# A fused two-block transformer on one core: the sparse attention's chain placed between its projection chunks, with convolution and weight splitting in one block ahead of the attention units

## Chip, cores and metric

The kernel runs on one core of a Trainium2 chip as a single launch. The metric is the device time of one execution in microseconds. Every number of a trace below is from one profiled execution; TensorE, VectorE, ScalarE and GpSimd are its compute engines, SP issues the weight loads.

## What is computed

The reference runs twelve stages on 256 tokens of width 1024: neighbourhood attention, dilated attention, a recurrent mixer with retention, two cross-attentions to a memory, a sparse attention with a short convolution, and six gated feed-forward layers, each between RMS norms. The change lies in the sparse attention stage. Cut to what matters:

```python
p = rms_norm(x) @ w_in      # 256 c_q | 128 c_kv | 64 k_idx | 8 w_idx | 3 x 512 h, gate_b, gate_c
c_q, c_kv = rms_norm_2(c_q, gq), rms_norm_2(c_kv, gkv)
q = einsum('btr,rhd->bthd', c_q, w_uq)
q_lat = einsum('bthd,hdc->bthc', q, w_uk)
q_idx = einsum('btr,rhd->bthd', c_q, w_qi)
score = einsum('bth,bths->bts', w_idx * 512 ** -0.5, relu(einsum('bthd,bsd->bths', q_idx, k_idx)))
# keep the 64 causal keys of highest score, softmax over them, values are c_kv
o = einsum('bthc,hcd->bthd', attend(q_lat, c_kv, top64(score)), w_uv)
u = gate_c * h                                   # short convolution, 3 taps over time
y = gate_b * (w0 * u[t-2] + w1 * u[t-1] + w2 * u[t] + b)
out = concat([o, y]) @ w_out
```

## The kernel before

**Weights.** All weight matrices lie in one stream of chunks of 128 x 2048 floats (1 MB). SP loads chunk after chunk into three slots of `raw`. ScalarE rounds a chunk to `whi` (`act_hi`, line 299; the "high part"), VectorE computes `wlo = raw - whi` (`dve_lo`, line 306; the "low part"; `half_lo`, line 312, does half of one). A product of full precision is then three matmuls: high x high, high weight x low input, low weight x high input (`mm3`, lines 230 to 232, and `mm3t`, lines 236 to 238, with the operands swapped). The slots are reused in a ring: ScalarE may write the high part of chunk c + 3 when TensorE has finished chunk c (`w_used`), VectorE then writes its low part and signals `w_lo`, for which TensorE waits before that chunk, and for which SP waits before it loads chunk c + 6 into `raw`.

**A stage.** Each stage has a projection (the chunks' products go to three banks `pj` in turn, VectorE evacuates a bank, scales it by the norm `rP` and frees it with `pj_free`), its own middle, and an output product `out_pe` over chunks with all four `acc` banks, followed by the post norm (`post_dve`) and the next stage's pre norm. `slices_pe` computes the first two chunks of a projection while the pre norm is still being made.

**The order of work** is written out by hand: each engine has a function that issues its instructions one after another (`pe_f`, `dve_f`, `act_f` of `dsa`), and counters of semaphores tie them together.

**The sparse attention stage** (`dsa`, lines 1223 to 1475). A projection chunk holds two tiles of 128 output columns, `tile_fm` for each half. Its nine chunks are: 0 and 1 (the three tiles of `c_q` and `c_kv` in `CQ`, and the index key written twice as `CK`), 2 (a tile with only eight columns, the index weights `WI`, by `few_tm`, and the first tile of `h`), 3 to 7 and the first half of 8 (the rest of `HB`: `h`, `gate_b`, `gate_c`). Behind the last of them comes a chain:

- ScalarE's squares `C2` (line 1430) are summed over partitions by TensorE with a column of ones (lines 1279, 1282); VectorE makes the variances (1357, 1358), GpSimd the roots (2300), TensorE spreads them (1287), VectorE normalises `CQ` (1374).
- TensorE makes index queries (1295) and the transposed keys (1301); ScalarE copies them out (1432); eight times TensorE makes two heads' index products (1311), ScalarE the ReLU (1445), VectorE the weighted sum into `SC` (1389, 1391).
- TensorE makes head queries (1295) and latent queries (1319), ScalarE copies them (1432, 1452).
- VectorE adds the causal mask (1397), takes the top 8 and replaces them eight times (1401, 1403) for two tiles of queries, and writes the mask `MBs` (1404, 1405).
- Between these, VectorE computes the short convolution: `gate_c * h` (1370), and for each of four tiles four operations (`conv`, 1363 to 1366); ScalarE makes the high parts of the result for the output product (1460).

Then `attn_pe`, `attn_dve` and `attn_act` run eight attention units (two heads and 128 queries each): scores, softmax, transposes of the weights, values. Their first scores wait for the mask. VectorE's `for k in range(8)` behind them (line 1412) makes the low parts of the output operand, four from the convolution and four from the attention's output (1332), which TensorE computes behind the first output chunk. The output product starts with the convolution's tiles. ScalarE issues the loads of the memory for the next stage (`mem_load`) ahead of the units.

## Time and profile before

| what | value |
|---|---|
| median of 3 runs | 2087.94 us |
| lowest, highest | 2085.4, 2097.81 us |
| the profiled execution's own time | 2086.02 us |
| its span, first to last instruction | 2084.2 us |
| mean granted TensorE clock | 0.983 |
| TensorE busy | 2003.8 us, 96% |
| VectorE busy | 1387.5 us, 67% |
| ScalarE busy | 944.2 us, 45% |
| chain that ended last | TensorE 86%, VectorE 9%, ScalarE 2% |

The page of a profile gives busy times by engine, a row of 40 equal slices of the span for each engine, and the chain of work that ended last. The granted clock is the share of TensorE's full speed. A timeline lists instructions in order of time; the idle time before one and what ended it stand in brackets. A table of stretches gives each engine's busy time between two moments. Matmuls overlap, so an instruction's length (0.28 us for a 256-column one) is longer than the distance to the next (0.11 us).

### The profile page before, as it was taken

The numbers are of one execution on the slowest core, as the hardware profiler recorded it, in microseconds if no ns is written. First come the engines' busy times: TensorE is split into PE (matmuls) and PEld (weight loads), VectorE is DVE, ScalarE is ACT, GpSimd is POOL, SyncE is SP. The second block draws the span as 40 slices with busy tenths as digits, with TensorE's granted clock in tenths as the row PEclk, the third lists the DMA queues.
The fourth block names the chain that finished last, engine by engine and source line by source line (L and its number), as shares of the span: only waits on it lengthen the run. The fifth ranks groups of instructions, "written<-read, shape, count | busy, mean of one in ns | idle before, by whom it ended". The sixth has DMA issues, their size and how long they took to land.

```text
span 2084.2 us, 37138 instructions
## 1 busy us (share of the span) xinstructions
PE 2003.8 (96%) x15066; PEld 1860.1 (89%) x15066; DVE 1387.5 (67%) x1853; ACT 944.2 (45%) x1258; POOL 33.2 (2%) x48
## 2 busy tenths in 40 slices
PE   7999999999999999999997999999999996999998
PEld 7879988999979988998997888998899895898997
DVE  6867756666767756775677575776577457666774
ACT  4554444443554444444344354444444443644442
POOL 0000000000000000000000010000000000000000
PEclk9999999999999999999999889999999998999999
DMA  7434564444415464555530223456455643143553
GB/s 299 153 115 182 198 214 173 179 162 152 153 72 202 182 225 151 200 183 211 205 131 16 87 93 131 171 192 215 159 193 190 219 177 134 52 162 112 189 201 124
DMA packets 49788, 341.46 MB, mean 164 GB/s; under 512 B 5776, under 2 KB 6544, under 8 KB 9616
## 3 DMA queue, kind: packets, MB, share of 16 engines
q1 hardware_dynamic: 45216, 321.21, 42.8%
q10 hardware_dynamic: 4464, 18.68, 2.4%
q8 instruction: 84, 1.38, 0.3%
q14 instruction: 24, 0.20, 0.0%
HBM read 338.82 MB, written 1.05 MB: 163 GB/s over the span
## 4 chain that ended last, share of the span: by engine, by line
PE 86%; DVE 9%; ACT 2%; issue 1%; POOL 0%; DMA 0%; DVEq 0%; SPq 0%; POOLq 0%; ACTq 0%
PE pj L230 15%; PE pj L232 15%; PE pj L231 15%; PE acc L236 7%; PE acc L238 7%; PE acc L237 7%; PE pj L236 2%; PE pj L238 2%; PE pj L237 2%; PE pj L571 2%; DVE wlo L306 2%; PE pj L577 1%; PE acc L638 1%; PE acc L651 1%; PE mb L662 1%
## 5 line engine op out<-in xcount | busy, mean ns | idle before, releaser
L306 DVE TENSOR_TENSOR wlo<-raw,whi 128x2048 fp32r<-128x2048 f32 x285 | 652.3, 2291 | 279.2 <-ACT whi L299 278.2
L230 PE MATMUL pj<-xh,whi 128*128 128x256 f32 x2704 | 753.3, 279 | 14.0 <-DVE wlo L316 12.8
L299 ACT ACTIVATE whi<-raw 128x2048 fp32r<-128x2048 f32 x299 | 569.6, 1911 | 399.1 <-PE acc L238 177.9
L231 PE MATMUL pj<-xl,whi 128*128 128x256 f32 x2704 | 749.5, 277 | 0.0
L232 PE MATMUL pj<-xh,wlo 128*128 128x256 f32 x2704 | 749.3, 277 | 0.0
L230 PEld LDWEIGHTS pj<-xh,whi 128*128 128x128 f32 x2704 | 510.1, 189 | 18.9 <-issue 15.5
L231 PEld LDWEIGHTS pj<-xl,whi 128*128 128x128 f32 x2704 | 509.8, 189 | 0.1
L232 PEld LDWEIGHTS pj<-xh,wlo 128*128 128x128 f32 x2704 | 509.7, 188 | 0.0
L236 PE MATMUL acc<-whi,AR 128*128 128x512 f32 x656 | 256.9, 392 | 2.4 <-DVE AR L777 2.3
L237 PE MATMUL acc<-whi,AR 128*128 128x512 f32 x656 | 255.8, 390 | 0.0
L238 PE MATMUL acc<-wlo,AR 128*128 128x512 f32 x656 | 255.7, 390 | 0.0
L832 ACT ACTIVATE AR<-F 128x256 f32 (+1 forms) x132 | 55.2, 418 | 374.4 <-DVE F L813 374.4
L236 PEld LDWEIGHTS acc<-whi,AR 128*128 128x128 f32 x656 | 123.6, 188 | 28.7 <-DVE AR L777 2.8
L238 PEld LDWEIGHTS acc<-wlo,AR 128*128 128x128 f32 x656 | 123.4, 188 | 25.9
L237 PEld LDWEIGHTS acc<-whi,AR 128*128 128x128 f32 x656 | 123.5, 188 | 25.1
L816 DVE TENSOR_TENSOR AR<-F,AR 128x256 f32 (+1 forms) x132 | 56.1, 425 | 100.8 <-ACT AR L832 100.8
L805 DVE TENSOR_TENSOR F<-pj,rP 128x512 f32<-128x512 f32 x132 | 90.4, 685 | 0.7
L236 PE MATMUL pj<-whi,xh 128*128 128x256 f32 (+1 forms) x304 | 85.8, 282 | 0.1
L238 PE MATMUL pj<-wlo,xh 128*128 128x256 f32 (+1 forms) x304 | 84.9, 279 | 0.0
L237 PE MATMUL pj<-whi,xl 128*128 128x256 f32 (+1 forms) x304 | 84.9, 279 | 0.0
L571 PE MATMUL pj<-xh,whi 128*128 128x256 f32 x320 | 82.4, 292 | 0.0
L571 PE MATMUL pj<-xh,wlo 128*128 128x256 f32 x320 | 78.1, 278 | 0.0
(358 smaller groups left out, 2355.3 us busy)
## 6 DMA issues: line engine op xcount, KB each, us to landing
raw<-in_wstream SPq DMA_DIRECT2D x302, 1024.0 KB, 4.8
F<-in_gains ACTq DMA_DIRECT2D x12, 512.0 KB, 4.3
F<-in_rpb ACTq DMA_DIRECT2D x3, 1024.0 KB, 4.8
XM<-in_memtok ACTq DMA_DIRECT2D x2, 1024.0 KB, 4.8
XM<-in_memin ACTq DMA_DIRECT2D x2, 1024.0 KB, 6.9
F<-in_small ACTq DMA_DIRECT2D x1, 1536.0 KB, 10.4
F<-in_xin SPq DMA_DIRECT2D x2, 512.0 KB, 6.1
xt<-in_xtok SPq DMA_DIRECT2D x1, 1024.0 KB, 12.0
```

Source lines behind the costliest of these rows:

```text
L230: nc.tensor.matmul(o, wh, k_hi, start=first, stop=False, skip_group_check=True)
L231: nc.tensor.matmul(o, wh, k_lo, start=False, stop=False, skip_group_check=True)
L232: return nc.tensor.matmul(o, wl, k_hi, start=False, stop=last, skip_group_check=True)
L236: nc.tensor.matmul(o, k_hi, wh, start=first, stop=False, skip_group_check=True)
L237: nc.tensor.matmul(o, k_lo, wh, start=False, stop=False, skip_group_check=True)
L238: return nc.tensor.matmul(o, k_hi, wl, start=False, stop=last, skip_group_check=True)
L299: nc.scalar.activation(whi[:, gs, :], raw[:, gs, :], ACT.Copy).then_inc(w_hi, 1)
L306: nc.vector.tensor_tensor(wlo[:, gs, :], raw[:, gs, :], whi[:, gs, :].bitcast(F32), ALU.subtract).then_inc(w_lo, 1)
L571: nc.tensor.matmul(o, a[:, (w.g + c) % 3, wk], xh[:, k, :], start=k == 0 and half == 0 and i == 0, stop=False, skip_group_check=True)
L805: nc.vector.tensor_tensor(GU.rearrange("p (a t) -> p a t", a=2), pj[ps][:, :].rearrange("p (a t) -> p a t", a=2), rP[:, None, :].to_broadc ...
L816: nc.vector.tensor_tensor(AR[:, bass.ds(c + FT, 1), :] if not isinstance(c, int) else AR[:, c + FT, :], M, (AR[:, bass.ds(c, 1), :] if not ...
L832: nc.scalar.activation(AR[:, bass.ds(c, 1), :] if not isinstance(c, int) else AR[:, c, :], M, ACT.Copy).then_inc(sg(tag, "hi2"), 1)
```

## The change

The projection has eight chunks. The index key (64 columns) and the index weights (8 columns) share one tile, `CR`, which is evacuated like the others; four small matmuls with slices of the identity take the key (once for each half of the partitions) and the weights out of it. `few_tm` is gone, and so is the ninth chunk, of which only a half was used.

The chain is issued by `behind(c, half)` between the halves of chunks 2 to 7: sums and extraction behind the first half of chunk 2, roots behind the first half of chunk 3, index queries behind chunk 3, two of the eight index products behind each half of chunks 4 and 5, head queries behind chunk 6, latent queries behind chunk 7. VectorE's and ScalarE's sequences are written out to match: evacuations (`evac`), low parts (`low`, for the chunk three ahead), scores, and the evacuations of chunks 6 and 7 behind the third and sixth top-8 round. The index products use the `acc` banks.

Between the mask and the softmax of the attention units, VectorE runs one block: the gate product, the four convolutions (their first operation is now ScalarE's, an Identity with scale and bias), the low parts of the first two output chunks in halves, and three low parts of the output operand. The low part of the third output chunk and the fourth of the operand follow the units.

```diff
-    return {"na": 12, "ffn": FT, "dil": 36, "rwrt": 15, "xa": 6, "dsa": 9}[kind]
+    return {"na": 12, "ffn": FT, "dil": 36, "rwrt": 15, "xa": 6, "dsa": 8}[kind]
...
-            dst_tiles = [CQ[:, 0], CQ[:, 1], CQ[:, 2], CK, None] + [HB[:, i] for i in range(12)] + [None]
+            dst_tiles = [CQ[:, 0], CQ[:, 1], CQ[:, 2], CR] + [HB[:, i] for i in range(12)]
...
+                def sums():
+                    pe.wait_ge(S("sq"), 3)
...
+                    for rows in (slice(0, 64), slice(64, 128)):
+                        nc.tensor.matmul(acc[1][rows, T:2 * T], ident[:, 0:64], CR, start=True, stop=True)
+                    for t in range(2):
+                        last = nc.tensor.matmul(acc[1][:, 8 * t:8 * t + 8], CR[:, t * P:(t + 1) * P], ident[:, 64:72],
+                                                start=True, stop=True)
+                    last.then_inc(S("st"), 1)
...
+                def behind(c, half):
+                    if (c, half) == (2, 0):
+                        sums()
+                    elif (c, half) == (3, 0):
+                        roots()
+                    elif (c, half) == (3, 1):
+                        index_queries()
+                    elif c in (4, 5):
+                        v_ = 4 * (c - 4) + 2 * half
+                        logits(v_)
+                        logits(v_ + 1)
+                    elif (c, half) == (6, 1):
+                        head_queries()
+                    elif (c, half) == (7, 1):
+                        latent()
+
+                slices_pe(pe, w)
+                for c in range(2, 8):
+                    pe.wait_ge(w_lo, w.g + 1)
+                    pe.wait_ge(pj_free, w.p + 1)
+                    for half in range(2):
+                        last = tile_fm(pj[w.p % 3], half, w.g % 3)
+                        if half:
+                            last.then_inc(w_used, 1)
+                        behind(c, half)
+                    w.g += 1
+                    w.p += 1
...
+                def evac(c):
                     dve.wait_ge(w_used, w.g + 1)
...
+                def low(c):
+                    dve_lo(dve, g0 + c, (g0 + c) % 3)
+
+                def low_half(c, part):
+                    if part == 0:
+                        dve.wait_ge(w_hi, g0 + c + 4)
+                        half_lo(dve, (g0 + c) % 3, 0)
+                    else:
+                        half_lo(dve, (g0 + c) % 3, 1).then_inc(w_lo, 1)
...
+                def conv(k):
+                    y = hb[:, k, :]
+                    dve.wait_ge(S("qlc"), 5 + k)
+                    link(dve, nc.vector.scalar_tensor_tensor(y, U[:, k, 1:T + 1], v("cw1", k), y, ALU.mult, ALU.add))
+                    link(dve, nc.vector.scalar_tensor_tensor(y, U[:, k, 2:T + 2], v("cw2", k), y, ALU.mult, ALU.add))
+                    nc.vector.tensor_tensor(y, y, bb[:, k, :], ALU.mult).then_inc(S("cv"), 1)
...
+                evac(0)
+                evac(1)
+                low(0)
+                dve.wait_ge(S("st"), 1)
+                link(dve, nc.vector.tensor_scalar(nt[:, 0:2], mb[:, 508:510], 1.0 / 256, EPS, ALU.mult, ALU.add))
+                nc.vector.tensor_scalar(nt[:, 2:4], mb[:, 510:512], 1.0 / 128, EPS, ALU.mult, ALU.add)\
+                    .then_inc(S("mv"), 1)
+                low(1)
+                evac(2)
+                low(2)
+                dve.wait_ge(S("bc"), 1)
...
+                dve.wait_ge(S("cn"), 3)
+                evac(3)
+                low(3)
+                nc.vector.memset(SC[:, 0, P:T], 0.0)
+                nc.vector.memset(U[:, :, 0:2], 0.0)
+                dve.wait_ge(S("qc"), 1)
+                score(0)
+                score(1)
+                evac(4)
+                score(2)
+                score(3)
+                low(4)
+                score(4)
+                score(5)
+                evac(5)
+                score(6)
+                score(7)
...
+                    if n in (2, 5):
+                        evac(6 if n == 2 else 7)
...
+                dve.wait_ge(pj_free, 3 + w.p)
+                nc.vector.tensor_tensor(U[:, :, 2:T + 2], cb_, hb, ALU.mult).then_inc(S("mask"), 1)
+                dve.wait_ge(S("mask"), 2)
+
+                def beside_units(i):
+                    if i < 4:
+                        conv(i)
+                    else:
+                        low_half(5 + (i - 4) // 2, i % 2)
+                        if i > 4:
+                            out_low(i - 5)
+
+                for i in range(8):
+                    beside_units(i)
+                attn_dve(dve, tag, units, 0, lambda grp: None)
+                out_low(3)
+                low(7)
+                for k in range(4, 8):
+                    out_low(k)
...
+                high = lambda: act_phase(act, w, 1, is_proj=True)
+                p0 = w.p
+                high()
+                high()
+                act.wait_ge(pj_free, 3 + p0 + 2)
+                for k in range(3):
+                    nc.scalar.activation(C2[:, k, :], CQ[:, k, :], ACT.Square).then_inc(S("sq"), 1)
+                act.wait_ge(S("st"), 2)
+                nc.scalar.activation(CK, acc[1][:, T:2 * T], ACT.Copy)
+                nc.scalar.activation(WI.rearrange("p a t -> p (a t)"), acc[1][:, 0:16], ACT.Copy, scale=512 ** -0.5)\
+                    .then_inc(S("qc"), 1)
+                high()
+                high()
+                act.wait_ge(S("q"), 1)
...
+                for v_ in range(4):
+                    relu(v_)
+                high()
+                for v_ in range(4, 8):
+                    relu(v_)
+                high()
+                high()
                 act.wait_ge(S("q"), 3)
                 copy_q(QT[:, 0:2], acc[1])
                 copy_q(QT[:, 2:4], acc[2])
+                high()
...
+                def beside_units(i):
+                    if i >= 4:
+                        k = i - 4
+                        act.wait_ge(S("cv"), k + 1)
+                        nc.scalar.activation(AR[:, 4 + k, :], hb[:, k, :], ACT.Copy).then_inc(S("oh"), 1)
+
+                mem_load(act, nmt)
+                act.wait_ge(S("mask"), 2)
                 for k in range(4):
-                    nc.scalar.activation(AR[:, 4 + k, :], hb[:, k, :], ACT.Copy).then_inc(S("oh"), 1)
-                mem_load(act, nmt)
+                    nc.scalar.activation(hb[:, k, :], U[:, k, 0:T], ACT.Identity, scale=v("cw0", k), bias=v("cb", k))\
+                        .then_inc(S("qlc"), 1)
+                for i in range(8):
+                    beside_units(i)
...
-    return ([fm_tile(W, 0), fm_tile(W, P), fm_tile(W, 2 * P), fm_tile(np.concatenate([kidx, kidx], axis=1), 0),
-             fm_tile(pad(W[:, 448:456]), 0)] + [fm_tile(W, 456 + i * P) for i in range(12)]
-            + [np.zeros((P, D), np.float32)])
-
+    return ([fm_tile(W, 0), fm_tile(W, P), fm_tile(W, 2 * P),
+             fm_tile(pad(np.concatenate([kidx, W[:, 448:456]], axis=1)), 0)] + [fm_tile(W, 456 + i * P) for i in range(12)])
```

On TensorE, before, the chain's first matmuls stand behind the last half chunk of the projection (`mb`, `acc`: accumulator banks; `cst`: constants; `F_51`: the stage's working memory; `nt`: the small tile of the variances and roots):

```order
L230 MATMUL pj<-xh,whi 128x256
L231 MATMUL pj<-xl,whi 128x256
L232 MATMUL pj<-xh,wlo 128x256
L1279 MATMUL mb<-cst,F_51 128x1 x4
L1282 MATMUL mb<-cst,F_51 128x1 x2
L1287 MATMUL acc<-cst,nt 128x128 x4
L1295 MATMUL acc<-F_51 128x256 x4
L1295 MATMUL pj<-F_51 128x256 x4
L1301 MATMUL mb<-cst,F_51 128x128 x2
L1311 MATMUL pj<-F_51 128x128 x3
```

In the change, the sums stand behind the first half of chunk 2, with the new extraction (lines 1276, 1278), and the next half chunk follows:

```order
L230 MATMUL pj<-xh,whi 128x256
L231 MATMUL pj<-xl,whi 128x256
L232 MATMUL pj<-xh,wlo 128x256
L1269 MATMUL mb<-cst,F_51 128x1 x4
L1272 MATMUL mb<-cst,F_51 128x1 x2
L1276 MATMUL acc<-F_51,cst 64x256 x2
L1278 MATMUL acc<-cst,F_51 128x8 x2
L230 MATMUL pj<-xh,whi 128x256
L231 MATMUL pj<-xl,whi 128x256
L232 MATMUL pj<-xh,wlo 128x256
```

What moved: the sums went from behind 12 half tiles to behind the first of them; the roots (line 1287, now 1285) come two half chunks later instead of next.

On VectorE, before, from the last low part of the projection to the normalised queries:

```order
L306 TENSOR_TENSOR wlo<-raw,whi 128x2048
L1357 TENSOR_SCALAR nt<-mb 128x2
L1358 TENSOR_SCALAR nt<-mb 128x2
L1368 MEMSET F_51 128x128
L1369 MEMSET F_51 128x4x2
L1370 TENSOR_TENSOR F_51<-F_51 128x4x256
L1363 TENSOR_SCALAR F_51<-F_51,vecs 128x256
L1364 SCALAR_TENSOR_TENSOR F_51<-F_51,vecs 128x256
L1365 SCALAR_TENSOR_TENSOR F_51<-F_51,vecs 128x256
L1366 TENSOR_TENSOR F_51<-F_51 128x256
L1374 SCALAR_TENSOR_TENSOR F_51<-F_51,vecs,acc 128x256 x3
```

In the change, from the first evacuation behind the pre norm to the clearing of `SC` and `U` (line 1372 is the evacuation, 297 the low part, 1421 and 1422 the variances, 1429 the normalised queries):

```order
L1372 TENSOR_TENSOR F_51<-pj,rP 128x256 x4
L297 TENSOR_TENSOR wlo<-raw,whi 128x2048
L1421 TENSOR_SCALAR nt<-mb 128x2
L1422 TENSOR_SCALAR nt<-mb 128x2
L297 TENSOR_TENSOR wlo<-raw,whi 128x2048
L1372 TENSOR_TENSOR F_51<-pj,rP 128x256 x2
L297 TENSOR_TENSOR wlo<-raw,whi 128x2048
L1429 SCALAR_TENSOR_TENSOR F_51<-F_51,vecs,acc 128x256 x3
L1372 TENSOR_TENSOR F_51<-pj,rP 128x256 x2
L297 TENSOR_TENSOR wlo<-raw,whi 128x2048
L1435 MEMSET F_51 128x128
L1436 MEMSET F_51 128x4x2
```

What moved: variances and normalisation now stand between evacuations and low parts; the convolution has left this place.

On VectorE, before, the mask's last two operations (1404, 1405) and the first units' softmax (1255 scales and masks the scores, 692 takes the row maxima):

```order
L1404 TENSOR_SCALAR F_51<-F_51 128x512
L1405 SCALAR_TENSOR_TENSOR F_51<-F_51 128x512
L1255 SCALAR_TENSOR_TENSOR Sb<-acc,F_51 128x256 x2
L692 TENSOR_REDUCE sm<-Sb 128x2
L1255 SCALAR_TENSOR_TENSOR Sb<-pj,F_51 128x256 x2
L692 TENSOR_REDUCE sm<-Sb 128x2
```

In the change, the end of the block ahead of the units: the last convolution (1406 to 1408), the half low parts (303) with those of the output operand (1414), and then the softmax (1247, 683):

```order
L1406 SCALAR_TENSOR_TENSOR F_51<-F_51,vecs 128x256
L1407 SCALAR_TENSOR_TENSOR F_51<-F_51,vecs 128x256
L1408 TENSOR_TENSOR F_51<-F_51 128x256
L303 TENSOR_TENSOR wlo<-raw,whi 128x2x512 x2
L1414 TENSOR_TENSOR AR<-F_51,AR 128x256
L303 TENSOR_TENSOR wlo<-raw,whi 128x2x512
L1414 TENSOR_TENSOR AR<-F_51,AR 128x256
L303 TENSOR_TENSOR wlo<-raw,whi 128x2x512
L1414 TENSOR_TENSOR AR<-F_51,AR 128x256
L1247 SCALAR_TENSOR_TENSOR Sb<-acc,F_51 128x256 x2
L683 TENSOR_REDUCE sm<-Sb 128x2
```

What moved: convolution, gate product, four half low parts and three of the operand's low parts stand between the mask and the first softmax.

## Rows read from the trace of the kernel before

**Rows 1.** Page: granted clock in 40 slices; one DMA issue.

```profile
PEclk9999999999999999999999889999999998999999
...
F<-in_small ACTq DMA_DIRECT2D x1, 1536.0 KB, 10.4
```

**Rows 2.** Stretches of the attention stage; first row names the columns.

```profile
core 0: us, PE busy (x) PEld busy (x) DVE busy (x) ACT busy (x) POOL busy (x), PEclk, DMA share, GB/s
1688.30:1701.70 13.40, 13.34 (x75) 13.26 (x75) 6.34 (x8) 4.19 (x6) 0.00 (x0) 0.62 0.72 277
1701.70:1731.40 29.70, 29.70 (x264) 29.70 (x263) 16.47 (x19) 11.53 (x6) 0.00 (x0) 1.00 0.46 170
1731.40:1741.80 10.40, 3.53 (x23) 3.15 (x21) 9.01 (x16) 1.91 (x1) 2.08 (x1) 0.67 0.59 225
1741.80:1761.60 19.80, 16.56 (x82) 12.07 (x82) 16.46 (x45) 6.76 (x21) 0.00 (x0) 0.92 0.00 0
1761.60:1772.00 10.40, 0.01 (x1) 0.00 (x0) 9.51 (x35) 3.28 (x8) 0.00 (x0) 0.69 0.51 202
1772.00:1796.80 24.80, 24.45 (x148) 21.34 (x149) 18.28 (x52) 15.08 (x43) 0.00 (x0) 0.92 0.00 1
```

**Rows 3.** TensorE timeline: start, length, engine, line, tiles, count [idle before <-releaser].

```profile
1732.22 0.58 PE L1282 MATMUL mb<-cst,F 128*128 128x1 f32 x4
...
1738.33 2.08 PE L1287 MATMUL acc<-cst,nt 128*128 128x128 f32 x8 [5.52 <-POOL nt L2300]
...
1752.35 1.25 PE L1311 MATMUL pj<-F 64*128 64x256 f32 x5 [0.29 <-ACT F L1445]
...
1753.75 3.72 PE L1295 MATMUL acc<-F 128*128 128x256 f32 x16
...
1758.65 2.96 PE L1319 MATMUL acc<-F 64*128 64x256 f32 x16 [1.18 <-ACT F L1432]
...
1772.05 2.05 PE L638 MATMUL acc<-F 128*128 128x256 f32 x4 [10.44 <-DVE F L1405]
...
1796.81 0.47 PE L236 MATMUL acc<-whi,AR 128*128 128x512 f32 x1
```

**Rows 4.** VectorE timeline, chain and mask.

```profile
1736.18 1.21 DVE L1370 TENSOR_TENSOR F<-F 128x1024 f32<-128x1024 f32 x1
...
1741.74 0.41 DVE L1363 TENSOR_SCALAR F<-F,vecs 128x256 f32<-128x256 f32 x1
...
1743.57 0.41 DVE L1363 TENSOR_SCALAR F<-F,vecs 128x256 f32<-128x256 f32 x1
...
1749.32 0.29 DVE L1389 TENSOR_SCALAR F<-F 128x128 f32<-128x128 f32 x1 [2.02 <-ACT F L1445]
...
1756.43 0.69 DVE L1397 TENSOR_TENSOR F<-F 128x512 f32<-128x512 f32 x1
...
1770.76 0.43 DVE L1404 TENSOR_SCALAR F<-F 128x512 f32<-128x512 f32 x1
...
1774.21 0.76 DVE L1255 SCALAR_TENSOR_TENSOR Sb<-acc,F 128x256 f32<-128x256 f32 x2 [2.31 <-PE acc L638]
```

**Rows 5.** VectorE timeline, behind the projection chunks.

```profile
1707.13 0.76 DVE L1351 TENSOR_TENSOR F<-pj,rP 128x256 f32<-128x256 f32 x2 [1.19 <-PE pj L232]
...
1709.09 2.29 DVE L306 TENSOR_TENSOR wlo<-raw,whi 128x2048 fp32r<-128x2048 f32 x1 [1.20 <-ACT whi L299]
...
1712.58 0.75 DVE L1351 TENSOR_TENSOR F<-pj,rP 128x256 f32<-128x256 f32 x2 [1.19 <-PE pj L232]
```

**Rows 6.** ScalarE timeline.

```profile
1687.75 3.71 ACT L299 ACTIVATE whi<-raw 128x2048 fp32r<-128x2048 f32 x2 [5.13 <-PE pj L577]
...
1692.68 1.03 ACT L1430 ACTIVATE F<-F 128x256 f32<-128x256 f32 x3 [1.23 <-DVE F L1351]
...
1763.58 1.35 ACT L1460 ACTIVATE AR<-F 128x256 fp32r<-128x256 f32 x4
```

More of the change, by code:

```diff
@@ L1227, in dsa @@
             C2 = take(3, T)
+            CR = take(T)
             CK = take(T)
@@ L1339, in dve_f @@
             def dve_f(dve, w):
-                for c in range(9):
+                g0 = w.g
+                def evac(c):
                     dve.wait_ge(w_used, w.g + 1)
@@ L1383, in dve_f, with score @@
+                def score(v_):
                     t, a = divmod(v_, 4)
```

169 lines of the change are left out of this document (59 added, 110 removed).

## The prediction, made before the changed kernel had run

> **What bounds the kernel now.** I read the page first, for where TensorE is short of work; then the table of stretches around the sparse attention stage; then the timelines of TensorE, VectorE and ScalarE there. All times below are microseconds of the profiled run's own clock.
>
> The page's row of granted clock [rows 1] stands at nine tenths or more except in three slices. The last of them holds the sparse attention stage. The stretches [rows 2] show it: after two projection chunks, the third takes 13.4 (1688.3 to 1701.7) at a granted clock of 0.62; the next 29.7 are dense at full clock; then come 10.4 with TensorE busy 3.5, 19.8 with 16.6 of small matmuls, 10.4 with nothing at all, and 24.8 of attention units. The last weight matmul of the projection ends at 1731.4 and the first one of the output product starts at 1796.8 [rows 3], so the chain and the units take 65.4.
>
> What ends last in that stretch alternates. TensorE waits 5.52 for GpSimd's roots and later 10.44 for the mask [rows 3]. The mask is VectorE's: eight rounds of top-8 and replace run from 1757.1 (behind the causal addition) to 1770.76, 13.6 or 1.70 a round, and another 1.3 passes until TensorE restarts at 1772.05 [rows 3, 4]. The softmax of unit 0 starts at 1774.21 [rows 4], and 22.6 later the output product starts.
>
> **Part by part: the projection.** A chunk takes 5.44 at full clock: evacuations behind consecutive chunks start at 1707.13 and 1712.58 [rows 5]; half a chunk is 2.72. Before, chunk 2 held the narrow product (48 matmuls of 8 columns) and a full half, and took 13.4; five chunks followed and a last half (2.7), together 43.1. Now six full chunks follow chunk 1: 6 x 5.44 = 32.6. That is 10.5 less weight work, of which the half clock made about half. The price is that the chain's matmuls now stand between the halves, so I walk TensorE from 1688.4.
>
> First half of chunk 2 to 1691.1. Then TensorE waits for the three squares: ScalarE's two conversions start at 1687.75 and take 3.71, and the squares 1.03 [rows 6], so to 1692.5. A stall of 1.4 that was not there. The sums of squares took 1.4 (1731.4 to 1732.8) [rows 3]. New: two 64-row matmuls of 256 columns and two of 8 columns that take the index key and weights out of one tile. The trace has no such pair; sixteen passes of a plain 256-column product take 3.72, 0.46 a matmul [rows 3], so 0.9 and 0.1 for the narrow ones is my upper end, and half of that the lower one if the two row halves overlap. I take 1.0.
>
> Then the rest, each from its row: the roots' spreading took 2.08 at half clock [rows 2, 3], 1.0 at full; the index queries 3.7 and two transposes 0.4 (half a 256-column matmul each); two index products of 256 columns 1.4 (1752.35 to the queries' start at 1753.75 [rows 3]) and two of 128 columns half of it, with 0.05 of handover each, so 4.4 for all eight; the head queries 3.72; the latent queries 2.96. With eleven halves (29.9) the sum from 1692.5 is 1.4 + 1.0 + 29.9 + 1.0 + 4.1 + 4.4 + 3.7 + 3.0 = 48.5: latent queries done at 1741.0, last projection matmul at 1738.0.
>
> **Does each handed-over step come in time?** VectorE now evacuates chunks 0 and 1 in one go, to 1690.4. The low part for chunk 3 is then done at 1692.7 and needed at 1697.7. GpSimd has the variances at 1694 and needs 2.1; the roots are at hand at 1696.1, TensorE asks at 1700.4: the 5.52 wait is gone. The low part of chunk 5 (2.29 [rows 5]) stands ahead of the normalised queries on VectorE: evacuation to 1698.4, ScalarE's conversion to 1699.6, low part to 1701.9, three products to 1703.3; TensorE asks at 1704.1. Slack 0.8, the thinnest. The small weights were issued in the norm before chunk 2 and take 10.4 [rows 1], so they are long landed. The low parts of chunks 6 and 7 are done at 1708.3 and 1720.0 and asked for at 1723.5 and 1732.7. SP's loads wait for low parts, three chunks ahead: the last one needed here is released at 1720, converted at 1738. The index scores take at most 0.9 each (eight in 7.1, 1749.32 to 1756.43, waits included [rows 4]) and nothing of them holds TensorE; they end 2 behind the last index products, at 1725.4, and the same conversions on ScalarE stand between the ReLUs without being late.
>
> VectorE then has the causal addition (0.7), three rounds, an evacuation, three rounds: 1737.1. Here it meets the new last wait: the evacuation of chunk 7 needs the matmul that ends at 1738.0. Evacuated at 1738.8, two rounds to 1742.2, mask at 1743.3. So TensorE's walk, not VectorE, sets the mask by 0.9. Before, the mask was at 1771.9: 28.6 earlier.
>
> **The block ahead of the units** takes part of that back, because the units' softmax is queued behind it on VectorE. It holds the gate product, 1.21 [rows 4]; ScalarE's first Identity, which the trace does not show: four 256-column copies took 1.35 and three squares 1.03 [rows 6], 0.34 either way, and 0.5 with the handover; four convolutions of three operations each. A four-operation convolution took 1743.57 - 1741.74 = 1.83 [rows 4], less its first 0.45 is 1.38, so 5.5. Then four half low parts, each half of 2.29, so 4.5, and three low parts of the output operand, 0.35 each by the like-sized evacuation (0.76 for two [rows 5]), 1.1. Sum 1.2 + 0.5 + 5.5 + 4.5 + 1.1 = 12.8: softmax at 1756.1 instead of 1774.2, 18.1 earlier. ScalarE's share (Identities, conversions) is beside it and has 4 to 5 to spare. The four output low parts that stood behind the units before were hidden by TensorE's last unit, so moving them ahead costs and returns nothing. The low part that now follows the units (2.29) is for the third output chunk, which TensorE reaches more than 11 later; VectorE sat idle there.
>
> The units: both first scores are done before the softmax asks, but TensorE has then been idle for about 10, as it had before 1772.0, where the clock was 0.69 and 0.92 after [rows 2]. Before, the two first scores absorbed the half clock ahead of the softmax; now scores 2, the fillers and the first transposes meet it. One unit's work is 2.6 of TensorE at full clock, of which 0.9 to 1.5 is met at half. I take 1.0. So the output product starts at 1756.1 + 22.6 + 1.0 = 1779.7, against 1796.8: 17.1 earlier. Everything behind is shifted whole: one chunk less in the stream changes slots, not the pace, and the memory load, issued 18 earlier, has no rival on its queue.
>
> The handovers inside the chunks are new, some ten of them, 0.05 each by what such handovers show without a wait: 0.6. **The sum: 16.5 less.** The profiled run took 2086.0 (span 2084.2), so it becomes 2069.5. The median of the runs shown is 1.9 above the profiled run; with it I say 2071.
>
> **The clock, weighed.** The clock fell during chunk 2's narrow product, although TensorE was busy all the time (0.62 over 1688.3 to 1701.7 [rows 2]), and came back only after dense matmuls had resumed. In 1741.8 to 1761.6, small products and short pauses, it was 0.92. After the change, about 3.8 of light work (stall, sums, extraction) stand between dense halves. If that makes it fall, the following half chunk and a bit run at half: 1.9 dearer, all on the path, since TensorE sets the mask. I give it four in ten and leave it out of the likeliest sum. The Trainium skill ("TensorE: Matmul & The Clock Gate", section "HAM oscillation — how this bites in real kernels") says that waits between bursts throttle the engine and that the transition is paid anew each time; that speaks against cutting a dense stretch with chain steps. The trace agrees where TensorE had nothing to do (0.69 in 1761.6 to 1772.0), and nothing in it shows a dense stretch cut so shortly. By the rule at its harshest the rival below results.
>
> **Rivals.** (1) Slower: the clock falls at chunk 2 and stays down because each further chunk is cut again. The 48.5 from 1692.5 then take 97; less the 16.5 gained it is 32 longer: 2120. It is slower from 16.5 of that stretch at half clock on. For it: the fall in chunk 2. Against: in chunks 6 and 7 the halves follow each other directly, and before, one dense half (5.4 at half clock, behind the narrow product) was enough to bring the clock back. (2) The gain is half: the thin handovers fail in turn (queries wait for the low part of chunk 5, scores for ReLUs behind a conversion), and each of about ten costs 0.8: 2071 + 8 = 2079. For it: VectorE and ScalarE each have a weight step of about 2 in front of a chain step, in their written order. Against: the slacks above are 0.8 to 12. (3) Better than forecast: extraction and roots at the lower end, no restart at half clock, VectorE 0.9 quicker than I have it: 3 more, and with a run as the profiled one as base 2066. (4) The change doesn't do what it says, as the block ahead of the units eats the mask's 28.6: it would have to hold 28, and its instructions sum to 12.8.
>
> **Chances.** Forecast with or without the one fall of the clock (2066 to 2076): 0.72; rival 1: 0.03; rival 2 0.14; rival 3 0.10; rival 4 0.01. A measurement of this kernel can tell about 1%, 21, from no change. The forecast stands at 17 below the median, inside that. Faster by over 1% needs below 2067: rival 3 and a little of the forecast, 0.15. Slower by over 1% is rival 1 and a bit: 0.04. Range 2062 to 2081.
>
> **What would show it.** Right: no stretch of 0.62 clock at the third chunk; the mask some 28 earlier and about 1 behind the last evacuation; then TensorE idle for 9 to 10 while VectorE is busy without a gap for 12.8; output product 65 less 17 behind where it began before. Wrong: VectorE waiting in its top-8 rounds for more than 2; waits of TensorE for the normalised queries; a clock of 0.5 reaching beyond chunk 3; the block longer than 14; or units that take over 24.

## The result, and the profile after

The changed kernel takes a median of 2078.0 us (2071.47 to 2083.26, 11 runs) against 2092.53 us of the kernel before beside it (2085.4 to 2099.41, 11 runs): a ratio of 0.9933, with an interval of 0.9913 to 0.9953. That is 14 us less, or 0.7%. The profiled run took 2076.19 us with a span of 2074.4, 9.8 less than before.

The page:

```profile
span 2074.4 us, 37066 instructions
...
PEclk9999999999999999999999989999999999999999
```

Three slices stood below nine tenths before [rows 1]; one is left, and that is not the sparse attention stage.

**A finer ruler than the whole run.** In this document "the stage" runs from TensorE's spreading of the norm ahead of chunk 2 to the first matmul of the output product. Before, it took 109.0 (1687.78 to 1796.81 [rows 3]); now 95.0 (1692.03 to 1787.04). The 14.0 agrees with the medians. The whole profiled run shows only 9.8 less because this one came to the stage 4.25 later, in code that is the same. It lost 4.23 of them in one feed-forward stage, where the granted clock is 1.00 in both runs: 190.33 (631.98 to 822.31) against 186.10 (631.54 to 817.64), with the same 1354 matmuls busy for 189.75 and 185.52. What made them slower stays open. Experiment e1, whose code is the same up to the stage, came 12.9 later: 4.3 of it in another feed-forward stage in the same way, and 8.2 in the recurrent stage, where the clock was lower (the kernel before first, then e1):

```profile
1100.00:1250.00 150.00, 137.63 (x1111) 126.88 (x1110) 105.82 (x166) 65.67 (x107) 5.90 (x6) 0.89 0.19 68
```

```profile
1100.00:1250.00 150.00, 135.98 (x1012) 124.64 (x1013) 99.03 (x157) 62.82 (x108) 5.19 (x5) 0.83 0.15 53
```

The columns are those of [rows 2]; the granted clock is the third number from the end. Six hundredths of 150 us are 9. Over all profiles here the stage starts between 1687.8 and 1700.7. So two single runs can't be told apart below some ten us, while a position inside the stage repeats to 0.3 where the clock is the same.

**The stage after, in stretches.** The first row names the columns:

```profile
core 0: us, PE busy (x) PEld busy (x) DVE busy (x) ACT busy (x) POOL busy (x), PEclk, DMA share, GB/s
1692.70:1696.70 4.00, 3.01 (x25) 2.81 (x25) 3.97 (x6) 3.93 (x5) 0.00 (x0) 1.00 0.93 380
1696.70:1700.10 3.40, 3.40 (x21) 2.63 (x21) 1.86 (x4) 0.00 (x0) 1.43 (x1) 0.69 0.74 218
1700.10:1705.30 5.20, 5.20 (x27) 5.20 (x28) 0.69 (x1) 0.46 (x2) 1.57 (x1) 0.54 0.78 274
1705.30:1744.90 39.60, 39.60 (x313) 37.21 (x313) 28.36 (x71) 15.80 (x26) 0.00 (x0) 1.00 0.23 81
1744.90:1753.40 8.50, 5.93 (x31) 4.64 (x29) 6.96 (x19) 5.55 (x9) 0.00 (x0) 1.00 0.48 182
1753.40:1765.10 11.70, 0.11 (x1) 0.00 (x0) 11.42 (x22) 2.18 (x7) 0.00 (x0) 0.61 0.37 141
1765.10:1787.00 21.90, 21.80 (x135) 19.51 (x136) 18.07 (x47) 14.96 (x43) 0.00 (x0) 0.89 0.11 46
```

They answer to [rows 2]. From chunk 3 on TensorE is busy without a gap for 39.6 at full clock, chain steps among it; the two stretches with 3.53 and 0.01 of TensorE's work are gone. In their place stands one, 11.7 long, with 0.11 of TensorE and 11.42 of VectorE: the block ahead of the units. What the forecast had not put in its sum are the second and third rows: 0.69 and 0.54 in chunk 2.

**TensorE's timeline**, answering to [rows 3]:

```profile
1692.03 0.60 PE L360 MATMUL mb<-cst,rsc 128*128 128x128 f32 x4
...
1696.68 1.05 PE L1269 MATMUL mb<-cst,F 128*128 128x1 f32 x8 [0.99 <-ACT F L1510]
1697.60 0.61 PE L1272 MATMUL mb<-cst,F 128*128 128x1 f32 x4
1698.14 1.12 PE L1276 MATMUL acc<-F,cst 128*64 128x256 f32 x4
1699.19 1.02 PE L1278 MATMUL acc<-cst,F 128*128 128x8 f32 x4
...
1707.84 1.05 PE L1285 MATMUL acc<-cst,nt 128*128 128x128 f32 x8
...
1745.14 2.96 PE L1317 MATMUL acc<-F 64*128 64x256 f32 x16
...
1750.68 1.10 PE L629 MATMUL acc<-F 128*128 128x256 f32 x4 [2.57 <-DVE F L1460]
...
1765.11 2.07 PE L629 MATMUL acc<-F 128*128 128x256 f32 x4 [11.60 <-DVE sm L683]
...
1787.04 0.47 PE L236 MATMUL acc<-whi,AR 128*128 128x512 f32 x1
```

The wait of 5.52 for the roots has no successor (line 1285 waits for nothing). The wait of 10.44 for the mask is now 2.57, but behind two units' scores TensorE waits 11.60 for the first softmax: the wait has changed its place more than its size. The third score at 1765.11 takes 2.07, where the second, like this one four matmuls of the same form, took 1.03 before the pause: the clock is at half when the units start.

**VectorE's timeline** from the last evacuation to the softmax, answering to [rows 4]:

```profile
1745.32 0.76 DVE L1372 TENSOR_TENSOR F<-pj,rP 128x256 f32<-128x256 f32 x2 [0.93 <-PE pj L232]
...
1749.38 0.43 DVE L1459 TENSOR_SCALAR F<-F 128x512 f32<-128x512 f32 x1
1749.84 0.69 DVE L1460 SCALAR_TENSOR_TENSOR F<-F 128x512 f32<-128x512 f32 x1
1750.57 1.22 DVE L1463 TENSOR_TENSOR F<-F 128x1024 f32<-128x1024 f32 x1
1752.53 0.49 DVE L1406 SCALAR_TENSOR_TENSOR F<-F,vecs 128x256 f32<-128x256 f32 x1 [0.74 <-ACT F L1551]
...
1758.04 2.35 DVE L303 TENSOR_TENSOR wlo<-raw,whi 128x1024 fp32r<-128x1024 f32 x2
...
1763.25 0.41 DVE L1414 TENSOR_TENSOR AR<-F,AR 128x256 fp32r<-128x256 f32 x1
1763.59 0.74 DVE L1247 SCALAR_TENSOR_TENSOR Sb<-acc,F 128x256 f32<-128x256 f32 x2
```

The top-8 rounds wait 0.93 for the last evacuation's matmul; the block then holds VectorE from 1750.57 to 1763.59, 13.0.

### The profile page after: what moved, and what is told of

Read it like the earlier page. It is cut to its first block, busy times and chain, and to the rows that moved or that the text cites. A ratio compares the mean times of both kernels' runs of the same rounds, so it can differ in the third digit from the quotient of the medians.

```text
span 2074.4 us, 37066 instructions
## 1 busy us (share of the span) xinstructions
PE 1999.3 (96%) x15026; PEld 1856.6 (90%) x15026; DVE 1382.8 (67%) x1848; ACT 944.4 (46%) x1263; POOL 34.1 (2%) x48
## 3 DMA queue, kind: packets, MB, share of 16 engines
q8 instruction: 84, 1.38, 0.3%
HBM read 337.77 MB, written 1.05 MB: 163 GB/s over the span
## 4 chain that ended last, share of the span: by engine, by line
PE 87%; DVE 9%; ACT 2%; issue 1%; DMA 0%; POOL 0%; DVEq 0%; SPq 0%; POOLq 0%; ACTq 0%
PE pj L230 15%; PE pj L231 15%; PE pj L232 15%; PE acc L236 7%; PE acc L238 7%; PE acc L237 7%; PE pj L236 2%; PE pj L562 2%; PE pj L237 2%; PE pj L238 2%; DVE wlo L297 2%; PE pj L568 1%; PE acc L629 1%; PE acc L642 1%; PE mb L653 1%
## 5 line engine op out<-in xcount | busy, mean ns | idle before, releaser
L297 DVE TENSOR_TENSOR wlo<-raw,whi 128x2048 fp32r<-128x2048 f32 x282 | 645.5, 2291 | 279.3 <-ACT whi L290 278.4
L238 PEld LDWEIGHTS acc<-wlo,AR 128*128 128x128 f32 x656 | 123.4, 188 | 25.6
L807 DVE TENSOR_TENSOR AR<-F,AR 128x256 f32 (+1 forms) x132 | 56.1, 425 | 100.8 <-ACT AR L823 100.8
L236 PE MATMUL pj<-whi,xh 128*128 128x256 f32 x288 | 80.8, 281 | 0.1
L238 PE MATMUL pj<-wlo,xh 128*128 128x256 f32 x288 | 80.0, 278 | 0.0
L237 PE MATMUL pj<-whi,xl 128*128 128x256 f32 x288 | 79.9, 278 | 0.0
```

The source lines that it names most:

```text
L236: nc.tensor.matmul(o, k_hi, wh, start=first, stop=False, skip_group_check=True)
L237: nc.tensor.matmul(o, k_lo, wh, start=False, stop=False, skip_group_check=True)
L238: return nc.tensor.matmul(o, k_hi, wl, start=False, stop=last, skip_group_check=True)
L297: nc.vector.tensor_tensor(wlo[:, gs, :], raw[:, gs, :], whi[:, gs, :].bitcast(F32), ALU.subtract).then_inc(w_lo, 1)
L807: nc.vector.tensor_tensor(AR[:, bass.ds(c + FT, 1), :] if not isinstance(c, int) else AR[:, c + FT, :], M, (AR[:, bass.ds(c, 1), :] if not ...
```

## Experiments

Each run is told by its place in the stage. The table gives, in us behind the spreading of the norm: the end of the projection (start of its last matmul), the end of the mask's last operation, the start of the first softmax and that of the output product, all from the timelines. Where two profiles differ in the fall of the clock in chunk 2, the difference of their rows holds that too; the section on the clock tells which do.

| kernel | projection | mask | softmax | output = stage |
|---|---|---|---|---|
| before | 43.5 | 84.1 | 86.4 | 109.0 |
| after | 52.9 | 58.5 | 71.6 | 95.0 |
| e1_eight_chunks | 33.3 | 74.7 | 77.0 | 99.6 |
| e2_sums_later | 48.6 | 54.2 | 67.3 | 91.2 |
| e3_fill | 49.9 | 55.5 | 68.6 | 92.4 |
| e4_full_tile | 36.0 | 77.6 | 79.9 | 102.7 |
| e5_no_low | 52.9 | 58.5 | 67.4 | 91.2 |
| e6_tail | 53.0 | 58.5 | 68.3 | 91.7 |
| e7_spread | 49.8 | 55.4 | 56.3 | 84.5 |
| e8_both | 48.6 | 54.2 | 56.1 | 84.4 |
| e9_product_first | 48.6 | 54.2 | 56.0 | 83.2 |
| e10_again | 51.4 | 57.0 | 70.0 | 93.1 |
| e11_again2 | 51.4 | 57.0 | 70.0 | 93.3 |
| e12_fill_again | 49.9 | 55.5 | 68.6 | 92.6 |

### What the removed chunk is worth

e1_eight_chunks is the kernel before with the new packing of the weights (index key and weights in one tile, eight chunks) and the extraction, but with the chain still behind the projection:

```diff
-"dsa": 9}[kind]
+"dsa": 8}[kind]
...
-                        if i == 4:
-                            last = few_tm(bank, half, slot, 8)
-                        elif i < 17:
-                            last = tile_fm(bank, half, slot)
+                        last = tile_fm(bank, half, slot)
...
+                for rows in (slice(0, 64), slice(64, 128)):
+                    nc.tensor.matmul(acc[1][rows, T:2 * T], ident[:, 0:64], CR, start=True, stop=True)
```

> The kernel before with one part of the change: eight chunks, the index key and weights in one tile and taken out by small matmuls, the whole chain still behind the projection, the old order on VectorE. The ruler is the stage in the trace, from TensorE's spreading of the norm (1687.8 before, 1692.0 after) to the first matmul of the output product: 109.0 before, 95.0 in the change. If the narrow product and its half clock made most of the gain, the projection is 10.5 shorter and the extraction adds 1 to 1.5: stage 99 to 100, time 9 to 10 below before, and interleaving the chain is worth only 4 to 5 of the change's 14. If interleaving is what pays, as the 28.6 earlier mask suggests, the stage is still above 103.

Measured: stage 99.6; 2090.44 us, a ratio of 0.997 (0.9923 to 1.0018). This profile came to the stage at 1700.66, the latest of all, which hides most of the gain in the whole time. TensorE behind its last half chunk:

```profile
1735.41 0.65 PE L1283 MATMUL acc<-F,cst 128*64 128x256 f32 x4
1735.99 0.61 PE L1285 MATMUL acc<-cst,F 128*128 128x8 f32 x4
...
1800.27 0.47 PE L236 MATMUL acc<-whi,AR 128*128 128x512 f32 x1
```

So 9.4 of the 14.0 come from one chunk less, 10.2 at the projection's end less the extraction and its handover. The placement of the chain and the block together bring 4.6: the mask comes 16.2 earlier than in e1, the block and what stands around it give 10.8 back, and the units take 0.8 longer.

e4_full_tile asks how much of the 9.4 is the narrow product. It puts a full tile in its place, so its index weights are not the right ones and it serves for the time alone:

```diff
-                            last = few_tm(bank, half, slot, 8)
+                            last = tile_fm(bank, half, slot)
```

> The kernel before with the narrow product (48 matmuls of 8 columns) replaced by 24 matmuls of 256 columns on the same tile; the index weights are then not what they should be, the work on them is the same. Chunk 2 then takes 5.4 for 13.4: stage 101, 8 less, the price of the narrow product with its half clock. Rival: the clock would have fallen there in any case: chunk 2 takes 8 or more.

Measured: stage 102.7; 2084.41 us, ratio 0.9945 (0.9891 to 0.9999). The projection ends 7.5 earlier than before, and the clock stays at 1.00 in chunk 2. A full tile is 24 matmuls of 256 columns, the narrow product 48 of 8 columns, and the trace before has them 0.11 apart at full clock: with nearly nothing to compute they cost twice a tile's time, and the clock fell besides. Of the 7.5, 1.2 were given back behind the projection, most of it where the chain's own phases of half clock fell on other matmuls (the second eight of the index queries took 2.75 instead of 1.89), which is why the expected 101 was missed.

### The clock in chunk 2

Two edits of the changed kernel. e2_sums_later moves sums and extraction behind the second half of chunk 2, where the squares are ready:

```diff
-                    if (c, half) == (2, 0):
+                    if (c, half) == (2, 1):
                         sums()
...
                 low(0)
+                low(1)
+                evac(2)
                 dve.wait_ge(S("st"), 1)
```

e3_fill leaves them, and gives TensorE three spare products in the wait:

```diff
                 def sums():
+                    for _ in range(3):
+                        nc.tensor.matmul(acc[2][:, 0:T], ident, cst[:, 0:T], start=True, stop=True)
                     pe.wait_ge(S("sq"), 3)
```

> The change with sums and extraction one half chunk later, behind the whole of chunk 2; ScalarE's two copies and VectorE's variances follow. Theory: in the change the wait for the squares (1.0) and 3.4 of light work let the clock fall and the next half chunk ran at half (5.25 for 2.72). Without the wait the light work is 2.4 and the clock stays: stage 95.0 - 1.0 - 1.0 - 2.5 = 90.5. Rival: the one-column matmuls alone are enough, as the narrow product was: the clock falls all the same, only the wait goes, stage 93 to 94.

> The change with three matmuls of 256 columns (results unused) in front of TensorE's wait for the squares, nothing else moved. They take 1.4 where 1.0 to 1.3 was a wait. If it was the idle wait that let the clock fall: no half clock in chunk 2, stage 91 to 92. If the one-column sums are enough: half clock as before, stage 95.

Measured: e2 91.2 (90.5 by the theory), 2070.58 us, ratio 0.989 (0.9846 to 0.9935). e3 92.4 (91 to 92 if the wait was to blame), 2080.02 us, ratio 0.9925 (0.9868 to 0.9981). Both profiles had a granted clock of 1.00 in chunk 2. But so had e7_spread (below), which has the changed kernel's code there, unaltered. Hence three more profiles:

> The changed kernel once more, unaltered, to see whether TensorE's clock falls in chunk 2 each time. Theory: the fall comes in some executions only; the stage takes 95.0 with it and about 91.9 without, and everything else in the stage keeps its place to 0.3. Rival: it falls whenever the wait for the squares, the sums and the extraction stand in one piece ahead of the second half of chunk 2, 95.0 each time; its absence in e7_spread then came from something else.

> The changed kernel unaltered, as e10_again. Theory: 95.0 with the fall, about 91.9 without it, and one of the two need not be that of e10_again. Rival: 95.0 each time.

> e3_fill once more, unaltered (three spare matmuls of 256 columns ahead of the wait for the squares). Theory (the fall comes in some executions, and the fill does not settle it): 92.4 without the fall or about 95.3 with it. Rival (the fill holds the clock): 92.4 with a granted clock of 1.00 in chunk 2 again.

Measured: e10 93.1 (one run, 2085.63 us), e11 93.3 (2082.26), e12 92.6 (2082.98). Sums, the half chunk behind them and what follows, in e10:

```profile
1702.30:1705.50 3.20, 2.21 (x19) 1.68 (x17) 1.68 (x4) 1.21 (x4) 0.00 (x0) 1.00 0.65 211
1705.50:1709.50 4.00, 4.00 (x22) 3.93 (x21) 2.15 (x1) 0.46 (x2) 2.99 (x1) 0.57 0.73 266
1709.50:1714.50 5.00, 5.00 (x46) 5.00 (x46) 2.65 (x3) 1.92 (x1) 0.00 (x0) 1.00 0.47 188
```

and in e12, with the fill:

```profile
1703.20:1706.40 3.20, 3.20 (x25) 2.67 (x23) 1.65 (x4) 1.17 (x4) 0.00 (x0) 1.00 0.65 207
1706.40:1710.40 4.00, 4.00 (x35) 3.93 (x34) 2.50 (x3) 0.81 (x3) 2.99 (x1) 1.00 0.68 250
```

In 4.0 us TensorE gets through 22 matmuls in the one and 35 in the other. Neither my theory (either the full fall or none) nor the rival (95.0 each time) foresaw this: the fall has a third size. For the fill the rival came, that it holds the clock (1.00, and 92.6 for 92.4). Over all profiles with the changed kernel's order in chunk 2 the projection ends at 52.9 or 53.0 (after, e5, e6: the fall begins with the extraction or just ahead of it and lasts nearly through the half chunk), at 51.4 (e10, e11: it begins with the half chunk and is over within it) or at 49.8 (e7: none). With the fill none of two profiles shows a fall, with the later sums none of three (e2, e8, e9). So the fall costs 3.1, 1.6 or nothing; five of six profiles had it in the changed order, none of five in the other two orders. That the stretch of waiting and light products allows it is shown as far as such counts go; what picks its size in one execution is open. The fill is worth 0.5 to 2.6, against 95.0 and 93.1; moving the sums is worth 1.2 to 1.4 more than it, as it takes the wait itself away.

In these orders the clock falls one pause later. The first score behind the mask follows a wait of 2.6 in e2, as in the changed kernel:

```profile
1743.84 2.04 PE L629 MATMUL acc<-F 128*128 128x256 f32 x4 [2.58 <-DVE F L1460]
```

It takes 2.04 to 2.07 in all five profiles of the two other orders, so it runs at half clock, and 1.10 to 1.13 in all six of the changed order. Why it falls there in the one case and not in the other isn't shown. From softmax to output product e2, e3 and e12 take 23.8 to 24.0, where the changed kernel, e10 and e11 take 23.1 to 23.4; that this comes of the later fall isn't shown either, as e5 (below) takes 23.9 with its first score at full clock.

### The block ahead of the units

e5_no_low leaves out the low parts of two weight chunks of the output product (it copies eight columns for each half), so two chunks of the output product lack a term; e6_tail keeps all work, but does chunk 5's low part whole ahead of the units and puts chunk 6's and the operand's four behind them:

```diff
-                for i in range(8):
+                for i in range(4):
                     beside_units(i)
+                low(5)
                 attn_dve(dve, tag, units, 0, lambda grp: None)
-                out_low(3)
+                for k in range(4):
+                    out_low(k)
+                low(6)
                 low(7)
```

> The change with the four half low parts of the block ahead of the units cut to copies of 8 columns each; the low parts of two output chunks are left out, so the output lacks them. Theory: the block is on the path with its whole length, because the softmax of the units is queued behind it and TensorE has nothing else: 4 x 1.13 less, 0.1 each for what stays: stage 95.0 - 4.1 = 90.9. Rival: the units are TensorE's, which is cold and would be late anyway: 93 or more.

> The change with part of the block moved behind the units: the low part of the second output chunk and the three low parts of the output operand. VectorE is idle for 2.9 between the last softmax and the output product and for 9 behind it, the second output chunk is needed 5.5 and its low part is there 3.7 after the softmax's end. Theory: 2.3 + 1.1 less ahead of the units, stage 91.6. Rival: the output product then waits for its operand or its weights, the gain is handed on: stage 94 to 95 with a wait at line 236.

Measured: e5 91.2 (one run, 2069.06 us) and e6 91.7 (2074.68 us, ratio 0.9924, 0.9893 to 0.9955), both with the full fall in chunk 2, as after. 90.9 and 91.6 were expected by the theory. VectorE in e6:

```profile
1754.54 2.28 DVE L297 TENSOR_TENSOR wlo<-raw,whi 128x2048 fp32r<-128x2048 f32 x1
1756.74 0.74 DVE L1247 SCALAR_TENSOR_TENSOR Sb<-acc,F 128x256 f32<-128x256 f32 x2
...
1763.39 0.76 DVE L1247 SCALAR_TENSOR_TENSOR Sb<-pj,F 128x256 f32<-128x256 f32 x2 [0.82 <-PE pj L629]
```

The block counts in full: 4.3 out of it in e5 brings the softmax 4.2 earlier and the output product 3.8, and 3.3 out of it in e6 brings 3.3. Behind the units there was room for all that e6 put there, since from the output product to the span's end e6 takes 287.3 and the changed kernel 287.4.

e7_spread empties the block: the gate product, the convolutions and one low part go between the units' steps on VectorE, ScalarE's share likewise, and the first two units' scores on TensorE wait for a bank instead of the mask. e8_both is e7 with e2's later sums:

```diff
-                pe.wait_ge(S("mask"), 1)
+                pe.wait_ge(pj_free, 3 + w.p)
                 attn_pe(pe, tag, units, 0)
...
-                for i in range(8):
-                    beside_units(i)
-                attn_dve(dve, tag, units, 0, lambda grp: None)
-                out_low(3)
+                    elif i < 5:
+                        conv(i - 1)
+                    elif i < 7:
+                        low_half(5, i - 5)
+
+                attn_dve(dve, tag, units, 0, lambda grp: None, beside_units)
+                for k in range(4):
+                    out_low(k)
+                low(6)
```

> The change with the block dissolved: gate product, convolutions and the low part of the first output chunk stand one after each unit, the rest behind the units as in the run before; TensorE's first scores wait for the evacuation of the last chunk and no longer for the mask. VectorE idles 4.2 between its mask and its last softmax in the change, TensorE 11.6 before its second scores. Theory: VectorE then bounds the units with 17.5 + 9.0 = 26.5 of its own, and 2.9 follow: output product 30 behind the mask where it was 36.5, stage 88.5. Rival: each piece delays the softmax that TensorE waits for, and the gaps fall on TensorE, stage 92 or more.

> Sums one half chunk later and the dissolved block together. Theory: the two are in different stretches and add: 95.0 - 4.5 - 6.5 = 84, time 25 below before (1.2%) and 11 below the change. Rival: VectorE's top-8 rounds bound the mask and take the first gain back: 88.

Measured: e7 84.5, 2071.04 us, ratio 0.99 (0.9872 to 0.9928); e8 84.4, 2066.61 us (2060.44 to 2071.24), ratio 0.9892 (0.9862 to 0.9921). e7 came out 4.0 better than expected: 3.1 is the fall in chunk 2 that this profile did not have, the rest my sum for the units. Less that 3.1, e7 brings 7.4 and e2 3.8, together 83.8; e8's 84.4 is near it, but beside e7 itself it is only 0.1 less, though its projection ends 1.2 earlier. The first score takes that back. In e7:

```profile
1753.32 1.13 PE L629 MATMUL acc<-F 128*128 128x256 f32 x4 [2.15 <-ACT F L1533]
```

It starts 55.1 behind the spreading of the norm at full clock; in e8 it starts at 53.9 and takes 2.07, and the softmax waits for it. In the whole time e8 is 21.0 below the kernel before beside it, where 25 was expected. In e8 TensorE also waits in the units where it did not in the changed kernel:

```profile
1743.01 2.07 PE L629 MATMUL acc<-F 128*128 128x256 f32 x4 [2.15 <-ACT F L1533]
...
1755.69 0.66 PE L642 MATMUL acc<-cst,F 128*128 128x128 f32 x4 [0.64 <-DVE F L693]
1759.17 0.66 PE L642 MATMUL acc<-cst,Sb 128*128 128x128 f32 x4 [0.63 <-DVE Sb L693]
1762.65 0.66 PE L642 MATMUL acc<-cst,Sb 128*128 128x128 f32 x4 [0.63 <-DVE Sb L693]
```

A unit takes 3.48 in place of 2.63, and VectorE sets it: two softmax parts and a convolution. The stage is shorter all the same, as a convolution, 1.38, costs 0.85 there and its whole length in the block, and behind the first scores the units run at full clock (1.00 from 1750 to 1773 in e8; 0.89 in the changed kernel's units).

e9_product_first takes the next piece: VectorE waits 1.92 for the first scores in e8, and the gate product fits in.

```diff
+                dve.wait_ge(pj_free, 3 + w.p)
+                nc.vector.tensor_tensor(U[:, :, 2:T + 2], cb_, hb, ALU.mult).then_inc(S("mask"), 1)
+
                 def beside_units(i):
-                    if i == 0:
-                        dve.wait_ge(pj_free, 3 + w.p)
-                        nc.vector.tensor_tensor(U[:, :, 2:T + 2], cb_, hb, ALU.mult).then_inc(S("mask"), 1)
-                    elif i < 5:
+                    if 0 < i < 5:
```

> As e8_both, with the gate product (1.21 us) ahead of unit 0's softmax on VectorE, in the 1.92 that VectorE waited there for the first scores in e8_both. Theory (VectorE sets the pace of the units, so each piece of its work counts unless it lies in a wait of its own): output product 1.2 earlier than in e8_both, stage 83.2 (84.4 before). Rival (TensorE's wait for ScalarE's copies of the latent queries and the first scores set it, so VectorE's place for the product makes nothing): 84.4 as before. Second rival: the product delays unit 0's softmax, because the scores come sooner than the wait shows: 85 or more.

Measured: 83.2; 2070.34 us (2062.37 to 2076.71), ratio 0.9898 (0.9862 to 0.9933).

```profile
1746.99 1.23 DVE L1463 TENSOR_TENSOR F<-F 128x1024 f32<-128x1024 f32 x1
1748.79 0.76 DVE L1247 SCALAR_TENSOR_TENSOR Sb<-acc,F 128x256 f32<-128x256 f32 x2 [0.58 <-PE acc L629]
```

The wait is 0.58 in place of 1.92 and the softmax stands where it stood (56.0 against 56.1), so the product has become free, and the output product is 1.2 earlier, as the theory had it and the rival of 84.4 had not. In the whole time 1.2 can't be seen: the intervals of e8 and e9 nearly coincide. Both beat the kernel before. Against the changed one their ratios overlap with its 0.9913 to 0.9953; what speaks for them is the stage, 10.6 and 11.8 shorter, of which 3.1 is the fall in chunk 2.

## Why the prediction was right, point by point

**The time.** 2071 was forecast, 2078.0 came, inside 2062 to 2081 and within 1% of no change. The forecast said 16.5 less and 14.0 came, so 2.5 is mine. The other 4.6 of the distance is the base: the kernel before had 2087.94 in the runs shown ahead of the forecast and 2092.53 beside the changed one.

**Projection: right, with one term left out.** Places are compared from the spreading of the norm. I had the last projection matmul ending at 50.2 with nothing for handovers and at 50.8 with 0.6 for them; where the clock does not fall (e7) it starts at 49.8 and takes 0.28. The terms hold: sums 1.4 (1.43 in e10, 1703.56 to 1704.99), extraction 1.0 (1.05 in e12, 1705.89 to the next weight matmul at 1706.94), roots' spreading not waited for. The stall for the squares was 1.2 in place of 1.4. The failed step is the one where I gave the fall of the clock in chunk 2 four in ten, priced it 1.9 and left it out: it came, in five of six profiles, and in the changed kernel's own it cost 3.1, which is more than the 2.5 by which the stage missed. The price was too low by my own rows: a half chunk is 2.72, and a half chunk "and a bit" at half clock costs that much again, not 1.9. And I let the fall begin with the dense half chunk: the extraction ahead of it was at half clock already and took 1.92 in place of 1.05 (1698.14 to 1700.06), and the half chunk took 5.06 in place of 2.72 (to 1705.12). The first of my signs of being right, no stretch of low clock at the third chunk, did not come.

**The Trainium skill on this** ("TensorE: Matmul & The Clock Gate", section "HAM oscillation — how this bites in real kernels") says that pauses between dense bursts throttle the engine, and that the price is paid each time anew. The trace agrees in that the clock fell in the long pause ahead of the units (0.61), as it did in every profile that has this pause. At the cut in chunk 2 the price was not the same each time: 3.1, 1.6 or nothing from run to run; there the measurement decides.

**Rival 1, that the clock stays down because chunks are cut again,** is out: from chunk 3 on it is 1.00 over 39.6. **Rival 2, that thin handovers fail,** is out too: no handover inside the chunks shows a wait of TensorE, and VectorE's one wait in the top-8 rounds is 0.93, where I had 0.9. It stands in every profile (0.92 in e9), whatever chunk 2 did, since TensorE's walk sets it. So the lost 3.1 went straight into the mask. Rival 3 (better than forecast) is out with the fall in chunk 2 and the half clock at the units, and rival 4 with a block of 13.0 and not 28.

**The mask** came 25.6 earlier (84.1 to 58.5); 28.6 was forecast, and 3.1 of it is chunk 2.

**The block: right.** 12.8 forecast, 13.0 measured. ScalarE's first Identity was undersized: four took 2.07, or 0.52 each, where I took 0.34 from copies and squares, and VectorE waited 0.74 for it, not 0.5. Convolutions (1.38) and low parts came as forecast, and e5 and e6 show that every piece of it counts.

**The units: right.** 1.0 forecast for the start at half clock, 0.8 measured (23.4 against 22.6 from softmax to output product). I had the place right too: the third score takes 2.07.

**Behind the stage** nothing changed: 287.4 from the output product's first matmul to the end of the span, before and after. One chunk less in the stream altered nothing there, as forecast. Other profiles show 287.3 to 291.8 for it, e10 with the changed kernel's own code among the longest.

## What to carry to other kernels

Products of a few columns can be as dear as wide ones (8 columns or 256, 0.11 a matmul here), and under them the clock fell: pack narrow outputs into a tile with others and take them out with one small product. This alone, with its fall of the clock, was two thirds of the gain here (9.4 of 14.0). When a chain is moved out from behind a dense stretch, ask what the freed wait lands on: a block that one engine does alone, ahead of units that need it, costs its full length, while between the units' steps its pieces meet that engine's waits. And where two versions differ by less than the whole run's scatter, measure between two landmarks of the trace around the change.

## What the runs showed of the hardware that I had not expected

- The clock fell with TensorE busy all the time, in the narrow product of the kernel before (0.62 over 13.4 [rows 2]). It did not in e4, with a full tile there, nor in e1, with nothing there (one profile each).
- The same instructions in the same order met a fall of three sizes (3.1, 1.6, 0 of lost time) in six profiles. A single profile can't tell whether an edit prevented it.
- Unchanged code moved the start of the stage by up to 12.9 between profiles (1687.8 to 1700.7). About two thirds of that is the clock in the recurrent stage. The rest arose in a feed-forward stage at a granted clock of 1.00: in seven of 14 profiles one such stage took 190.3 to 191.0 in place of 186.1 to 186.9. What slowed it is open.
- With the light work filled or moved, the clock held in chunk 2, and fell instead at the next pause of 2.2 to 2.6 (first score 2.04 to 2.07 for 1.10 to 1.13).
- The two 64-row products of 256 columns and the two of 8 columns, two passes each, take 1.05 together: the narrow ones are again nearly as dear as the wide ones (0.58 and 0.47 between starts in e12).
- Two thirds of the added work on VectorE per unit reached the end (0.85 of 1.38), though TensorE had been without a gap there: its slack behind VectorE was 0.5 a unit.
